# High parts of the turned feature tiles read from the PSUM banks, their low parts on VectorE alone, and reordered matmuls around both mixer tails

## The reference

```python
for layer in range(DEPTH):
    mix = _even_mixer(x, ...) if layer % 2 == 0 else _odd_mixer(x, ...)
    x = _layer_norm(ALPHA * x + mix, ln1_g[layer], ln1_b[layer])
    x = _layer_norm(ALPHA * x + _swiglu(x, w_gate, w_up, w_down), ln2_g[layer], ln2_b[layer])
```

## Time and profile before

| what | us |
|---|---|
| median of three runs | 1258.07 |
| the profiled execution's own time | 1257.68 |
| its span, first to last instruction | 1255.9 |
| TensorE (PE) busy | 1232.8 |
| TensorE weight loads (PEld) busy | 1011.2 |
| GpSimd (POOL) busy | 602.8 |
| VectorE (DVE) busy | 449.1 |
| ScalarE (ACT) busy | 442.0 |

### The profile page before, as it was taken

How to read it: one execution, slowest core, us unless ns; L and a number is a source line. 1 busy time by engine, 2 the same in 40 slices (tenths; PEclk the granted TensorE clock), 3 DMA queues, 4 the chain that set the end, 5 groups by cost and what they waited for, 6 DMA issues and landing times.

```text
span 1255.9 us, 17125 instructions
## 1 busy us (share of the span) xinstructions
PE 1232.8 (98%) x7112; PEld 1011.2 (81%) x7112; DVE 449.1 (36%) x769; ACT 442.0 (35%) x661; POOL 602.8 (48%) x292
## 2 busy tenths in 40 slices
PE   9999998999999999999999999999999999999997
PEld 7878776888888888886777889887688888888885
DVE  5557526311111000127778845663621111010105
ACT  4167724222222221214544456542422222221111
POOL 4243444944444343446743347444694444435341
PEclk9999999999999999999999999999999999999999
DMA  9221041333233233231344243124133233323231
GB/s 321 91 68 68 23 147 44 124 102 99 75 97 98 87 126 124 101 101 48 103 116 120 75 127 94 27 69 134 34 107 109 86 101 101 101 84 135 83 101 67
DMA packets 106065, 122.96 MB, mean 98 GB/s; under 512 B 18947, under 2 KB 80581, under 8 KB 105989
## 3 DMA queue, kind: packets, MB, share of 16 engines
q1 hardware_dynamic: 98244, 118.56, 29.7%
q10 hardware_dynamic: 7744, 3.32, 1.0%
HBM read 117.93 MB, written 3.70 MB: 97 GB/s over the span
## 4 chain that ended last, share of the span: by engine, by line
PE 91%; DVE 4%; DVEq 2%; POOL 1%; issue 1%; ACT 1%; ACTq 0%
PE bank L1661 27%; PE bank L1663 27%; PE bank L1662 27%; PE bank L2062 3%; DVEq L471 2%; DVE f_ab L1174 1%; POOL w_lo L681 1%; DVE stats L1236 1%; DVE x_tm L1234 1%; PE bank L2171 1%; PE bank L1722 1%; PE bank L1894 1%; PE bank L2008 0%; PE bank L2154 0%; DVE x_tm L1197 0%
## 5 line engine op out<-in xcount | busy, mean ns | idle before, releaser
L681 POOL TENSOR_TENSOR w_lo<-w_raw,w_hi 128x1024 fp32r<-128x1024 f32 (+1 forms) x200 | 469.9, 2371 | 525.7 <-ACT w_hi L823 525.5
L1661 PE MATMUL bank<-x_hi,w_hi 128*128 128x512 f32 x880 | 344.3, 391 | 0.0
L1662 PE MATMUL bank<-x_lo,w_hi 128*128 128x512 f32 x880 | 342.5, 389 | 0.0
L1663 PE MATMUL bank<-x_hi,w_lo 128*128 128x512 f32 x880 | 342.5, 389 | 0.0
L823 ACT ACTIVATE w_hi<-w_raw 128x1024 fp32r<-128x1024 f32 (+1 forms) x200 | 196.3, 1032 | 210.0 <-issue 161.3
L1661 PEld LDWEIGHTS bank<-x_hi,w_hi 128*128 128x128 f32 x880 | 165.2, 188 | 35.2 <-issue 0.8
L1663 PEld LDWEIGHTS bank<-x_hi,w_lo 128*128 128x128 f32 x880 | 165.2, 188 | 34.4
L1662 PEld LDWEIGHTS bank<-x_lo,w_hi 128*128 128x128 f32 x880 | 165.2, 188 | 34.0
L1243 DVE TENSOR_TENSOR f_ab<-bank,f_ab 128x512 f32<-128x512 f32 x44 | 30.4, 692 | 363.7 <-PE bank L1663 363.7
L1663 PE MATMUL bank<-w_hi,h_lo 128*128 128x512 f32 x352 | 136.9, 389 | 0.0
L1661 PE MATMUL bank<-w_hi,h_hi 128*128 128x512 f32 x352 | 136.9, 389 | 0.0
(11 more groups left out here) (284 smaller groups left out, 1243.3 us busy)
## 6 DMA issues: line engine op xcount, KB each, us to landing
w_raw<-ffn_w_gate_dram SPq DMA_DIRECT2D x22, 1024.0 KB, 5.4
w_raw<-ffn_w_up_dram SPq DMA_DIRECT2D x22, 1024.0 KB, 5.3
w_raw<-ffn_w_down_dram SPq DMA_DIRECT2D x20, 1024.0 KB, 5.0
w_raw<-od_w_in_dram SPq DMA_DIRECT2D x16, 1024.0 KB, 5.9
w_raw<-ev_w_in_dram SPq DMA_DIRECT2D x8, 1024.0 KB, 5.6
w_raw<-ev_w_out_dram SPq DMA_DIRECT2D x4, 1024.0 KB, 5.2
w_raw<-od_w_out_dram SPq DMA_DIRECT2D x4, 1024.0 KB, 5.2
x_fm<-x_fm_dram SPq DMA_DIRECT2D x8, 256.0 KB, 6.8
```

The lines of the kernel that those rows point to most:

```text
L681: pool.tensor_tensor(w_lo[:, b % 2, c], w_raw[:, b % 2, c], w_hi[:, b % 2, c].bitcast(F32), ALU.subtract).then_inc(w_lo_ready, 1)
L1661: pe.matmul(out_ap, st[0], mv_[0], start=start, stop=False)
L1662: pe.matmul(out_ap, st[0], mv_[1], start=False, stop=False)
L1663: return pe.matmul(out_ap, st[1], mv_[0], start=False, stop=stop)
```

## The change

Four edits. (1) `round_x`: ScalarE makes `x_hi[2..7]` from the banks, with a gain and a bias per partition, and also `f_ab` of tiles 3, 5 and 7; VectorE makes `f_ab` of tiles 1, 0, 2, 4, 6 and all eight `x_lo`; GpSimd makes none and waits for the last of them before its second piece of low weights. (2) `fm_block(fresh)` takes tiles 0 and 1 together for each output bank. (3) Layer 0's tail issues both fillers' matmuls on high weights before those on low weights for k = 4 to 7 too; layer 1's tail has more filler work ahead of the transposes, splits the two transposed halves, and moves VectorE's filler between the heads' halves. (4) `tm_group` of half 1 starts with the high weights of its first two k for all tiles (`late=2`).

```diff
-            def low_parts(i):
-                for k in range(1, KD, 2):
-                    pool.wait_ge(s["x_hi_ready"], KD * i + k + 1)
-                    pool.tensor_tensor(x_lo[:, k, :], f_ab[:, k % 4, :], x_hi[:, k, :].bitcast(F32), ALU.subtract)\
-                        .then_inc(s["x_lo_odd"], 1)
...
                     split_lo(b + 1, (0,))
-                    low_parts(turned[b])
+                    low_part_there(pool, turned[b], KD - 1)
...
-                for k in range(1, KD):
-                    taken(act, ("xT", i, k))
-                    act.activation(x_hi[:, k, :], f_ab[:, k % 4, :], ACT.Copy).then_inc(s["x_hi_ready"], 1)
+                taken(act, ("xT", i, 1))
+                act.activation(x_hi[:, 1, :], f_ab[:, 1, :], ACT.Copy).then_inc(s["x_hi_ready"], 1)
+                for k in range(2, KD):
+                    full(act, ("xT", i, k))
+                    scale, bias = (lnc[:, c + k:c + k + 1] for c in (gcol, gcol + 16))
+                    act.activation(x_hi[:, k, :], bank(("xT", i, k))[:, :], ACT.Identity, scale=scale,
+                                   bias=bias).then_inc(s["x_hi_ready"], 1)
+                    if k % 2:
+                        if k > 4:
+                            low_part_there(act, i, k - 4)
+                        take(act.activation(f_ab[:, k % 4, :], bank(("xT", i, k))[:, :], ACT.Identity, scale=scale,
+                                            bias=bias), ("xT", i, k))
...
-                for k in (1, 0, *range(2, KD)):
+                for k in (1, *range(0, KD, 2)):
                     full(dve, ("xT", i, k))
-                    if k == 0:
-                        dve.wait_ge(s["x_hi_ready"], KD * i + 1)
+                    if k != 1:
+                        dve.wait_ge(s["x_hi_ready"], KD * i + k + 1)
...
-                    if k % 2 == 0 and k > 0 or k == KD - 1:
-                        low((k - 1) // 2 * 2)
+                    if k != 1:
+                        low(k)
+                        low(k + 1)
...
                 ins.then_inc(s["o_odd"], 1)
-            filler(NT - 1, 3)
+                if hg == 0:
+                    filler(NT - 1, 3)
...
+                def high(k, n):
                     weights_there(b, k)
                     pe.wait_ge(s["x_hi_ready"], KD * fresh + k + 1)
+                    ps, w, x = fill(keys[n]) if k == 0 else bank(keys[n]), weights(b, k, n * P, P), xcols(k, ALL)
+                    pe.matmul(ps[:, :], w[0], x[0], start=k == 0, stop=False)
+                    pe.matmul(ps[:, :], w[1], x[0], start=False, stop=False)
+                for k in range(KD) if fresh is not None else ():
                     for n in range(len(keys)):
+                        if k == 0:
+                            high(0, n)
+                            high(1, n)
+                        elif k > 1:
+                            high(k, n)
...
+                    for kk in range(late) if k0 == 0 else ():
+                        if kk % (nk // 2) == 0:
+                            pe.wait_ge(w_hi_ready, split_count(b, kk // (nk // 2)))
+                        wait_k(kk)
+                        for t in tiles:
+                            ps = fill((*name, t)) if kk == 0 else bank((*name, t))
+                            hi = weights(b, kk, 0, width)[0]
+                            pe.matmul(ps[:, 0:width], src(kk, tile_cols[t])[0], hi, start=kk == 0, stop=False)
+                            pe.matmul(ps[:, 0:width], src(kk, tile_cols[t])[1], hi, start=False, stop=False)
+                    for kk in range(late) if k0 == 0 else ():
+                        weights_there(b, kk)
+                        for t in tiles:
+                            pe.matmul(bank((*name, t))[:, 0:width], src(kk, tile_cols[t])[0], weights(b, kk, 0, width)[1],
+                                      start=False, stop=False)
...
-                if key[0] == "mix" and k0 == 0:
-                    for i in range(2):
+                if key[0] == "mix":
+                    for i in range(k0 // 4, (k1 + 3) // 4):
                         taken(pe, turned(key[1], key[-1], i))
...
-                tm_group(("mix", layer, 1), have, in_turn=True)
+                tm_group(("mix", layer, 1), have, in_turn=True, late=2)
...
-            for key in TAIL_FILLERS[0]:
-                tile_of(key, 4, 8)
+            for low in (False, True):
+                for key in TAIL_FILLERS[0]:
+                    part_of(key, 4, 8, low)
...
-            tile_of(ahead, 0, 4)
-            turn_o(1, NT - 1)
-            tile_of(ahead, 4, 7)
+            tile_of(ahead, 0, 6)
+            turn_o(1, NT - 1, (0,))
+            tile_of(ahead, 6, 8)
+            turn_o(1, NT - 1, (1,))
             tile_of(last, 0, 4)
-            tile_of(ahead, 7, 8)
             tile_of(last, 4, 8)
```

More of the change, by code:

```diff
@@ L1687, in fm_block @@
                 steps = [(n, k) for n in range(len(keys)) for k in range(KD)]
-                for k in range(KD) if fresh is not None else ():
+                def high(k, n):
                     weights_there(b, k)
                     pe.wait_ge(s["x_hi_ready"], KD * fresh + k + 1)
-                    x = xcols(k, ALL)
+                    ps, w, x = fill(keys[n]) if k == 0 else bank(keys[n]), weights(b, k, n * P, P), xcols(k, ALL)
+                    pe.matmul(ps[:, :], w[0], x[0], start=k == 0, stop=False)
+                    pe.matmul(ps[:, :], w[1], x[0], start=False, stop=False)
+                for k in range(KD) if fresh is not None else ():
                     for n in range(len(keys)):
[L1693 to L1696, removed]
+                        if k == 0:
[3 more added lines that the diff above has]
+                            high(k, n)
                     for kl in [k - 2] * (k > 1) + [KD - 2, KD - 1] * (k == KD - 1):
@@ L1725, in few_columns, with tm_group @@
                 done(ins, key)
-            def tm_group(name, wait_k, src=xcols, kt=KD, in_turn=False, tiles=range(NT), pair_last=False):
+            def tm_group(name, wait_k, src=xcols, kt=KD, in_turn=False, tiles=range(NT), pair_last=False, late=0):
                 b = first_block[name]
@@ L1737, in tm_group @@
                         steps = [(kk, t) for t in tiles for kk in range(nk)]
-                    waited = -1
-                    for kk, t in steps:
+                    waited = late - 1 if k0 == 0 else -1
+                    for kk in range(late) if k0 == 0 else ():
[12 more added lines that the diff above has]
+                                      start=False, stop=False)
+                    for kk, t in [(kk, t) for kk, t in steps if kk >= late or k0]:
                         if kk > waited:
@@ L1799, in part_of @@
                     if low:
-                        pe.matmul(ps[:, :], x_hi[:, k, x], lo, start=False, stop=False)
+                        ins = pe.matmul(ps[:, :], x_hi[:, k, x], lo, start=False, stop=k == KD - 1)
+                        if k == KD - 1:
+                            done(ins, key)
                     else:
@@ L1818, in turn_x, with turn_o @@
                             done(ins, ("xT", i, k))
-            def turn_o(layer, t):
-                for i in range(2 if layer else 1):
+            def turn_o(layer, t, parts=(0, 1)):
+                for i in parts if layer else (0,):
                     if layer == 0:
```

## The result

The changed kernel takes 1243.62 us (median of 4 runs, 1243.39 to 1244.32) beside 1258.09 for the kernel before (4 runs, 1258.04 to 1260.04) on the same chip: a ratio of 0.9882, interval 0.9865 to 0.9899, or 14.5 us less. 1244.6 was forecast. The profiled execution took 1243.55 us, its span 1241.7. TensorE is busy 1227.7 us of it (1232.8 before, since the longer first matmul after each wait counts as busy too) and idle for 14.0 us instead of 23.1.

A forecast was written before the change was run, and what follows sets the result against it. TensorE, busy 1232.8 of 1255.9 us, was taken as the bound. Savings 3.35 + 3.1 + 3.0 + 2.5 + 1.6 = 13.5 us off the profiled 1257.68 gave 1244.2, plus 0.4 for the median 1244.6; range 1242.4 to 1249.8.

The forecast's parts named there:

- Turns: The three 48-matmul stages from round_x: each 11.35 us long, so 3.35, 3.1 and 3.0 us less.
- tail 0: End of layer 0: high-weight matmuls first remove two waits for low weights, transposes at 160.4, 2.5 us less.
- tail 1: End of layer 1: waits for VectorE's output and low weights go, half 1 starts at 855.35, 1.6 us less.
- ScalarE's evaluations: In a turn: eight evaluations at 0.80 us bring x_hi[7] at 208.2, wanted at 210.3, margin 2.1 us.
- The bounds of 0.63 and 0.85: In a turn: ScalarE's second evaluation of the same bank, absent from the trace, lies between these us; 0.78 taken.
- VectorE's rounds: In a turn: three rounds of one f_ab and two low parts, 2.25 us each; x_lo[7] at 210.65, margin 1.5 us.
- the loss at 202.18: Turn 1: TensorE's wait for tile 0's bank, which goes since the bank is wanted at 202.5 and taken at 202.13.
- The wait on GpSimd: Behind turn 1: GpSimd's held low-weight piece is there at 213.1, wanted at 215.4; cost nothing.
- Turns pay half: Rival, chance 0.10: in the turns TensorE runs into ScalarE or VectorE tile by tile, about 1.6 a turn; 1249.2.
- tails pay nothing: Rival, chance 0.07: in both tails waits move behind VectorE's filler and the last piece of low weights; 1248.6.
- The change doesn't do what it says: Rival, chance 0.04: GpSimd's held-back pieces or affine work come late for the feed-forward blocks; anywhere up to 1254.
- VectorE becomes the bound: Rival, chance 0.03: in the turns low parts of 1.7 us give 1264; at 1.4 us each, the time before, 1258.

The follow-up runs named there:

- fab_ahead: `hi_from_fab` with VectorE making its f_ab ahead of its low parts, by pairs; 1248.45 us (ratio 0.9926).
- odd_low_gpsimd: Changed kernel with low parts of tiles 1, 3, 5, 7 back on GpSimd, its held piece behind them; 1243.53 us (0.9885).
- bank_hi_alone: Changed kernel with all f_ab on VectorE and odd low parts on GpSimd; ScalarE still makes high parts from the banks; 1248.32 us (0.9923).
- no_hold: Changed kernel without GpSimd's wait for the last low part before its second piece of low weights; 1257.77 us (0.9998).
- double_low: Changed kernel with each of the turns' twenty-four low parts computed twice in a row on VectorE; 1262.05 us (1.0026).
- hi_from_fab: Changed kernel with all f_ab on VectorE and ScalarE copying x_hi[1..7] from it; low parts stay on VectorE, GpSimd held; 1255.39 us (0.9978).
- tail0_undone: Changed kernel with layer 0's two fillers in whole products for k = 4 to 7 again; 1245.89 us (0.9902).

## Why the prediction came out

**Turns: 9.97 us, 9.45 foretold.** The waits for `x_hi` are gone as argued; the size is off by 0.22, 0.08 and 0.22 us. The third matmul starts 0.58 behind the first, not 0.65, and from there the matmuls take 0.229 us with no restart, where the sum took 0.23 and 0.1. This gain was put too small, and it is 0.5 of the 0.7 us between the sum of 13.5 and the 14.2 measured; tail 0, put too large, and tail 1, too small, nearly cancel. The median is 1.0 us below the forecast: besides these 0.7, the forecast added 0.4 for the distance of a median from the profiled execution, which came out at 0.07.

**ScalarE's evaluations.** 0.80 us each was taken: eight of them take 6.51 us, from 199.52 to 206.03, 0.81 each. The bounds of 0.63 and 0.85 held. The margin is 1.8 us instead of 2.1, about half of it since TensorE is quicker and half since ScalarE is slower than taken.

**VectorE's rounds.** 2.25 us foretold, 2.33 measured: the drain is 0.17 to 0.19 and the steps between add some. The margin came out at 1.1 us, 1.5 foretold. That only the first low part would meet GpSimd is right, at 1.70 for two.

**What was incomplete in the argument on the turns.** I put the old loss down to VectorE's low part standing still beside GpSimd's, and left it at that. That the collision costs time is borne out: `fab_ahead` keeps all `f_ab` on VectorE, has no GpSimd low parts, and its turns take 37.5 us instead of 43.5, with the pairing of the first two tiles and a new order in it. But it is not the only way out, and `odd_low_gpsimd` shows that beside the other edits the move of the low parts isn't needed: the same time, with collisions still there. What gives then is that high parts come from the banks, past VectorE (`bank_hi_alone`: three turns in 38.1 us, the pairing included), and that ScalarE takes three `f_ab` off VectorE's round (38.1 to 33.5). The pairing is 0.3 a turn of this, the loss at 202.18 that the forecast names. The sum wasn't hurt by naming only the one cause; a shorter version of the change would have been misjudged.

**The wait on GpSimd costs nothing.** Right: the held piece is there at 211.02, and TensorE, now in its next block at 210.13, wants it twelve matmuls on, at 212.85. The margin is 1.8 us, 2.3 foretold. What the forecast didn't price is what the wait saves: 14.15 us (`no_hold`), once all low parts are VectorE's.

**Tail 0: 2.36 us, 2.5 foretold**, with the transposes at 160.59, where 160.4 was written down. The eight low matmuls at the start take 2.06 us, not the 1.84 of the sum. Undone alone it costs 2.07 by the start of turn 1, 2.39 counted from the tail's own first row (152.77 there, 153.09 here), and 2.27 by the medians.

**Tail 1: 1.71 us, 1.6 foretold**, half 1 starting 12.93 us after the row that answers to 842.32, 13.0 foretold. Its two parts are 1.0 for the reordering and 1.2 for the late weights. Transposes 4.89 and 6.71 us behind the start, 4.83 and 6.8 foretold. VectorE's chain, whose filler now stands between the two fours of heads, has them done at 839.91, 0.05 us before the second transposes: in time, but only just.

**Rivals.** *Turns pay half* (1249.2) and *tails pay nothing* (1248.6) are excluded by 9.97 and 4.25. *The change doesn't do what it says*: no wait for GpSimd's low weights is left at all. *VectorE becomes the bound* isn't what happens, with low parts of 0.74 us in the mean; but the mechanism is real. `double_low` comes to 1262.05, with a little under 1.4 us for the two operations of each low part, where the rival had the time before reached at 1.4. By the rival's own terms 1.4 gives a round of 3.78 us, as measured, but only 1256.8 us; the time before is reached at about 1.45. The run is 5 us above the 1256.8, and 3.5 of them are lost behind the turns, most of it to the lower clock, which the rival didn't count.

## What to carry to other kernels

Compare the round of the slowest helper with the round of the bounding engine for the same tiles (here 2.99, then 2.33 us, beside 2.73): once it is below, moving more work gains nothing, and the margin is what a new collision must eat first. Where two engines can stand in each other's way, the one with slack can be held back explicitly: with all low parts on VectorE that one line carried as much as the whole change. But look first for a split that needs no such line, as `odd_low_gpsimd` here. Where the granted clock falls behind a long wait, ask what the next late operand is before its price is written down: in turn 1 of `hi_from_fab` 1.6 us of slow matmuls cost 0.1, since a later tile was late anyway; behind turns 1 and 3 of `double_low` nothing else was late, and 1.6 us were lost each time.

## What the runs showed of the hardware

- TensorE's granted clock fell to its lower level behind waits of 1.97 us (`hi_from_fab`) and of 1.65 and 0.58 us within 2 us (`double_low`), and matmuls of 512 columns then followed each other at 0.43 instead of 0.23 us, for 3.9 us in the first case. Behind the wait of 1.12 us before the change, and of 1.22 in `tail0_undone`, the granted clock stayed at 1.00, and so it did behind turn 2 of `double_low`, after the same 1.65 and 0.58. The length of a wait alone doesn't tell it.
- GpSimd's operations get longer too beside VectorE's low parts: 2.71 and 2.84 us instead of 2.39, and 3.45 for two low parts instead of 2.58. Neither engine comes out of a collision unharmed.
- The same instructions reach turn 1 at times up to 1.4 us apart from kernel to kernel, in one profiled execution each; the four runs of the changed kernel differ by 0.9.
